# A two-layer decoder trunk on one core: where the forget columns stand in the SyncE queue, and from which count the first three weight loads may start

## What is computed

```python
cond = jax.nn.silu(c)
mod = cond @ w_mod[l] + b_mod[l]                 # (2048) @ (2048, 12288)
sh1, sc1, g1, sh2, sc2, g2 = jnp.split(mod, 6, axis=-1)
h = modulate(rms_norm(x, norm_gain[l, 0]), sh1, sc1)
proj = h @ w_in                                  # w_in: (2048, 3 * 2048 + 8)
q, k, v = proj[..., :3 * D] ...                  # 16 heads of 128
f_logit = proj[..., 3 * D:] + b_forget           # the eight forget columns
```

## Time and profile before

| what | us |
|---|---|
| median of 3 runs | 2072.96 (2072.81 to 2076.98) |
| the profiled execution, whole | 2075.47 |
| its span (first to last instruction) | 2073.9 |
| TensorE busy in it | 2005.1 (97%) |
| VectorE busy | 1655.8 (80%) |
| ScalarE busy | 1054.7 (51%) |
| GpSimd busy | 307.4 (15%) |

### The profile page before, as it was taken

The page is one execution under the profiler, slowest core; times in us unless marked ns, Lnnn a source line. Parts: engine busy times, 40 slices in busy tenths (PEclk is TensorE's granted clock), DMA queues, the critical chain, the costliest instruction groups (busy, mean ns, idle before and its releaser), DMA issues.

```text
span 2073.9 us, 33153 instructions
## 1 busy us (share of the span) xinstructions
PE 2005.1 (97%) x12242; PEld 1792.9 (86%) x12242; DVE 1655.8 (80%) x2321; ACT 1054.7 (51%) x1551; POOL 307.4 (15%) x459
## 2 busy tenths in 40 slices
PE   3999999999999999999999999899999999999998
PEld 2888989888999889999899987688888888888886
DVE  5777899987899998998989986898965666666665
ACT  4323764554555544555445555555543555434553
POOL 3332342220121122111211210011100000000000
PEclk8999999999999999999999999999999999999999
DMA  9999899886789899888998884297765555555552
GB/s 360 355 353 328 305 330 333 298 298 215 257 314 333 319 353 343 321 317 295 353 358 303 313 305 143 88 336 268 262 203 184 194 190 184 199 186 192 194 184 101
DMA packets 235851, 558.39 MB, mean 269 GB/s; under 512 B 14024, under 2 KB 15032, under 8 KB 235192
## 3 DMA queue, kind: packets, MB, share of 16 engines
q1 hardware_dynamic: 180408, 355.03, 49.4%
q0 software_dynamic: 55296, 201.35, 27.3%
HBM read 554.23 MB, written 2.10 MB: 268 GB/s over the span
## 4 chain that ended last, share of the span: by engine, by line
PE 86%; DVE 6%; issue 3%; DMA 3%; ACT 2%; POOL 0%; DVEq 0%; POOLq 0%; ACTq 0%
PE ps L680 15%; PE ps L704 10%; PE ps L706 10%; PE ps L705 10%; PE ps L655 8%; PE ps L657 8%; PE ps L656 8%; PE ps L685 8%; PE ps L724 3%; DVE w_lo L1522 2%; DVE macc L1536 2%; DMA mraw<-in_w_mod 1%; PE ps L721 1%; DMA early<-in_w_mod 1%; ACT work L1108 1%
## 5 line engine op out<-in xcount | busy, mean ns | idle before, releaser
L1108 ACT ACTIVATE w_hi<-raw 128x1024 fp32r<-128x1024 f32 x640 | 668.3, 1057 | 726.6 <-PE ps L706 242.1
L1522 DVE TENSOR_TENSOR w_lo<-raw,w_hi 128x1024 fp32r<-128x1024 f32 x640 | 767.2, 1226 | 296.4 <-ACT w_hi L1108 295.3
L655 PE MATMUL ps<-h_pair,w_hi 128*128 128x256 f32 x1792 | 513.9, 287 | 2.0 <-DVE w_lo L1522 1.6
L656 PE MATMUL ps<-h_pair,w_hi 128*128 128x256 f32 x1792 | 508.5, 284 | 0.0
L657 PE MATMUL ps<-h_pair,w_lo 128*128 128x256 f32 x1792 | 508.4, 284 | 0.0
L1536 DVE SCALAR_TENSOR_TENSOR macc<-mraw,cond,macc 128x512 f32<-128x512 f32 x620 | 427.9, 748 | 47.8 <-DMA mraw<-in_w_mod 39.9
L540 POOL DMA_DIRECT2D mraw<-in_w_mod x358 | 258.8, 723 | 1170.9 <-DVE macc L1536 874.9
L655 PEld LDWEIGHTS ps<-h_pair,w_hi 128*128 128x128 f32 x1792 | 345.1, 193 | 4.8 <-issue 4.7
L656 PEld LDWEIGHTS ps<-h_pair,w_hi 128*128 128x128 f32 x1792 | 345.1, 193 | 1.3 <-issue 1.2
L657 PEld LDWEIGHTS ps<-h_pair,w_lo 128*128 128x128 f32 x1792 | 344.9, 192 | 0.0
L680 PE MATMUL ps<-h_pair,w_hi 128*128 128x512 f32 x1408 | 340.5, 393 | 1.1 <-DVE w_lo L1522 1.0
(11 more groups left out here) (177 smaller groups left out, 1511.5 us busy)
## 6 DMA issues: line engine op xcount, KB each, us to landing
mraw<-in_w_mod POOLq DMA_DIRECT2D x358, 512.0 KB, 6.2
raw<-in_w_up SPq DMA_DIRECT2D x176, 1024.0 KB, 6.1
raw<-in_w_down SPq DMA_DIRECT2D x88, 1024.0 KB, 5.9
raw<-in_w_attn_in SPq DMA_DIRECT2D x48, 1024.0 KB, 8.3
raw<-in_w_attn_out SPq DMA_DIRECT2D x16, 1024.0 KB, 7.2
work<-in_w_mod POOLq DMA_DIRECT2D x12, 512.0 KB, 8.8
early<-in_w_mod POOLq DMA_DIRECT2D x8, 512.0 KB, 12.8
raw<-in_w_pool SPq DMA_DIRECT2D x4, 1024.0 KB, 5.1
```

The costliest lines, as they stand in the source:

```text
L655: mm(o, wh, ah, start=st, stop=False, skip_group_check=True)
L656: mm(o, wh, al, start=False, stop=False, skip_group_check=True)
L1108: return nc.scalar.activation(o, i, f, **kw)
L1522: V.tensor_tensor(w_lo[:, s, :, :], raw[:, j % 4, h * 1024:(h + 1) * 1024].rearrange("p (k n) -> p k n", k=2), w_hi[:, s, :, :].bitcast(F3 ...
```

## The change

The loads of `wf` and `bfb` are taken out of the loop over positions, where they stood ahead of position 4, and put ahead of position 0, directly behind the last parameter load. The loads at positions 0, 1 and 2 wait for `mod_acc` at 16, 20 and 24 in place of 22, 24 and 26: for VectorE to be through with pieces 1, 3 and 5 of chunk 1, where before it had to be through with pieces 4, 5 and 6.

```diff
+            with nc.allow_non_contiguous_dma("the eight forget columns, the bias on every partition"):
+                sp.dma_start(wf[:, :, :], w_attn_in[0, :, 3 * D:3 * D + NF]
+                             .rearrange("(k p) n -> p k n", p=P)).then_inc(s_wf, 16)
+                sp.dma_start(bfb[:, :], b_forget[0:1, :].to_broadcast([P, NF])).then_inc(s_wf, 16)
+
             def load(q, j, src):
 
                 if isinstance(q, int) and q == 0:
-                    sp.wait_ge(mod_acc, (22, 24, 26, 34)[j])
+                    sp.wait_ge(mod_acc, (16, 20, 24, 34)[j])
                     if j >= 2:
                         sp.wait_ge(x_t, 8)
...
             for pos in range(48):
-                if pos == 4:
-                    with nc.allow_non_contiguous_dma("the eight forget columns, the bias on every partition"):
-                        sp.dma_start(wf[:, :, :], w_attn_in[0, :, 3 * D:3 * D + NF]
-                                     .rearrange("(k p) n -> p k n", p=P)).then_inc(s_wf, 16)
-                        sp.dma_start(bfb[:, :], b_forget[0:1, :].to_broadcast([P, NF])).then_inc(s_wf, 16)
```

## The result

The changed kernel takes 2079.18 us (median of 22 runs, 2075.32 to 2084.99), the kernel before, on the same chips, 2074.22 us (median of 22). The ratio is 1.0022, interval 1.0016 to 1.0028: 4.6 us slower, between 3.3 and 5.8. The forecast was 4.6 us slower. One of the 22 runs of the kernel before took 9860.24 us; a median is hardly moved by it. The profiled execution took 2079.26 us against 2075.47, 3.8 us more, with a span of 2077.7 us.

The account below looks back on a forecast made before the run. TensorE, 97% busy, was taken as the bound, its stream starting when the load at position 0 lands. A start at 49.0 in place of 44.39 adds 4.6 us to the median 2072.96: 2077.6 us, 8 in 10 between 2072.9 and 2080.4.

Parts of the forecast that it names:

- Start of the stream: TensorE's first L724, released by the load at position 0: at 49.0 us (47.4 to 50.5), 4.6 us later than 44.39.
- the level engines' 47.4: Landing of the load at position 0 if all engines are level: 44.7 us plus 2.7 us for 1.05 MB, +3.0.
- The lag of 2.0 us: In q0 some engine runs 2.0 us behind, so the load at position 0 lands there at 49.4 us.
- Packets in turn: Engines take one packet from q0 and q1 in turn, whatever its size; 136 small ones each, 0.183 us a turn.
- rival A: Small loads in q1 go in bundles, stream starts 4.1 us earlier, 2068.9 to 2070.9 us; chance 0.12.
- The counts at 0: Earlier wait of the load at position 0: alone at most 4.3 us gained, with the small loads ahead 0.
- The hold of SyncE: Issue of `bfb` holds SyncE's queue from about 11 us to between 33 and 42; cost 0.
- Chunk 2 and the load at position 3: VectorE's wait for piece 4 goes from 3.66 us to about 1; load at position 3 up to 6 us later.
- a cover of 13: Slack before the first product of the load at position 3, behind TensorE's sum at 69.46: 13 us against 6.
- The clock: Low level at TensorE's start rises a like time behind it, so the delay counts full 4.6 us, not half, 2.3.
- Handed on whole: Between 170 and 230 us VectorE follows TensorE, not the transfers, so a later start is passed on in full.
- rival C: The delay is given back through slack or the clock: +1 to +2.5 us, about 2075 us; chance 0.08.

Follow-up runs that it names:

- e3_half: Changed kernel with 8 of 16 rows of `wf` per partition ahead of position 0, the rest and `bfb` ahead of position 4; ratio to kernel before 1.0008.
- e2_move: Changed kernel with the old counts 22, 24, 26, so only `wf` and `bfb` are moved; ratio to the kernel before 1.0021 (1.0013 to 1.0030).
- e1_counts: Kernel before with only the counts changed to 16, 20, 24, `wf` and `bfb` still ahead of position 4; ratio 1.0015 (1.0006 to 1.0023).
- e5_bias_first: Changed kernel with `bfb` issued ahead of `wf` in place of behind it; one run, no ratio, first L724 at 48.94 us.
- e9_pos3_old: Kernel before with `wf` and `bfb` ahead of position 3 in place of 4, counts 22, 24, 26 kept; ratio 1.0010 (1.0001 to 1.0019).
- e6_act: Changed kernel (counts 16, 20, 24) with `wf` on ScalarE's queue at the head of its program, `bfb` ahead of position 0; ratio to kernel before 0.9993.
- e4_quarter: Changed kernel with 4 of 16 rows of `wf` per partition ahead of position 0, the rest and `bfb` ahead of position 4; ratio to kernel before 0.9994.

## Why the prediction was right

*Start of the stream.* Forecast 49.0 (47.4 to 50.5), measured 49.15 in the changed kernel, 49.18 and 48.94 in two others with all packets ahead. The choice of a time near the slowest engine's over the level engines' 47.4 was right, but two terms of the sum were off by about as much in opposite directions, so part of the closeness is luck. For the slow engine the sum has the last run at 46.7 and the load 2.7 us behind it. By the packets of the changed kernel's trace, the last run moves at 45.2, and the load lands 3.9 us behind it. The lag of 2.0 us was read from a landing: in the kernel before q0's last packet moves at 49.2 and lands at 50.0, so 0.8 of the 2.0 is no engine's delay but the way from a last packet to its landing.

*Packets in turn.* Right, and now direct: 905 to 905. The rule of the Trainium skill that was rival A (DMA: Bandwidth & Descriptors, section Queues, rings and completion order: some 9 to 17 descriptors from one ring before switching) doesn't hold for these transfers; by it, as an estimate from the page, 136 small packets would take 8 to 15 turns, at 0.183 us a turn less than 3 us, and `wf` landed at 45.3, 18.9 us behind the parameters' last packet (26.4). The measurement decides. One size was off: I counted a turn as 0.183 us, for q0's packets of 4 KB alone. The rows have 905 turns on 16 engines in 9 us, 0.159 us each, since q0's packets of 4 bytes (104 of the 905) are turns too. There are more turns for as much less time, so the end of q0 doesn't move, but what stands ahead of a load is worked off faster: this is the 1 us by which e3_half was forecast too late (its 64 runs an engine were to end at 38.2 and end at 36.9).

*The counts at 0.* Right in this kernel (e2_move). The value I gave them alone, up to 4.3 us at the start, was right for the start (39.84) and wrong for the end, as e1_counts shows; the prediction didn't rest on it.

*The hold of SyncE.* Forecast to end between 33 and 42 and to cost nothing: it ended at 33.4, and e5_bias_first shows the nothing (48.94 in place of 49.15). That holds for a hold ahead of position 0; in e9_pos3_old, ahead of position 3, one does cost.

*Chunk 2 and the load at position 3.* VectorE's wait for piece 4 was to go from 3.66 to about 1 and went to 0. The load at position 3 was to come up to 6 us later and came 5.9 later, under a cover of 13; no wait of TensorE came of it.

*The clock.* Taken at the full value and not at half: the granted clock rises at 53.7 us, 4.5 us behind the start, and at 49.7 in the kernel before, 5.3 us behind it (the prediction had read 5.7). So of 4.8 us 4.4 are left behind position 1.

*Handed on whole.* Right for a delay: +4.6 in e5_bias_first at every point to 131 us, and +4.4 at 480. The changed kernel's own profile went back to 2.9, because it didn't have the stretch at low clock at 70.6, and to 3.7 later. The range of the timed ratio, 3.3 to 5.8 us, holds the 4.6. This is not rival C: what came back was that stretch at low clock, which isn't in all profiles of either kind, not slack.

The same step would have been wrong for a gain. Of the six profiles (five kernels) whose stream starts at 39.8 to 41.3 only one, e6_act's, kept 3 us, and the second profile of the same kernel kept 0.9. From 60 to 131 us the modulation's chunks and the loads at 3 and 4 follow the transfers, not TensorE, with 13 us or less in hand, and TensorE waits 0.9 to 3.2 us for a chunk in the other five. Where a wait is followed by the low clock, it costs a second time, as the rows at 84 and 120 us show. What sets the other short stretches at low clock (70, 238, 299, 973, 1112 us in some executions) stays open; each is worth some 1.5 us, which is part of what executions of one kernel differ by.

## What to carry to other kernels

A transfer of many short runs is cheap in bytes and costs one turn a run: ahead of a wanted load, on the same queue and beside a full one, count packets per engine, not KB, and price each at the other queue's packet. Leave out those that are gone before the load would move its own first packet, and those that run when the other queue is empty. Put such a transfer where the engines are still empty, on a queue nothing urgent follows on; directly behind the last small loads was the worst of the places tried, since another queue had filled the engines by then. And ask of a gain at the start what else must come earlier for it to last: a delay is handed on by itself, a gain only if every supplier has the slack.

## What I had not expected of the hardware

One us of idle TensorE in the first 130 us can cost twice. In e4_quarter it waits 1.3 us in 116 to 119.2 us, and the next 3.4 us run at a granted clock of 0.57, which costs about as much again. Over all profiles TensorE waits nine times for the sum of chunk 3 or 5. Seven of these waits (1.1 to 3.2 us) have a stretch at the low level beginning 0.6 to 2.2 us behind them; two (0.9 us in e4_quarter, 1.1 us in e9_pos3_old) have none. Between 79 and 131 us no profile has such a stretch without such a wait. No run changed the wait alone, so this is what goes together, not a shown cause.

Not all engines had the same queue ahead. In 10 to 26.5 us q1 moved 1476 packets in the changed kernel and 1122 in the one before: 354 more packets went by while the parameters were still on their way, so some engines were done with the parameters much earlier.

```profile
q0 software_dynamic: 1528, 5.58, 91.8%
q1 hardware_dynamic: 1476, 0.51, 12.7%
```

The Trainium skill (DMA: Bandwidth & Descriptors, section Why a DMA increments its semaphore by 16 and not by 1) says that a DMA is spread over the largest number of engines up to 16 that divides its slowest dimension; for the eight loads of 88 rows that would be 11, with five engines left out. e4_quarter agrees with its numbers. Of its 512 runs ahead of position 0, 32 on each engine, 160 (5 times 32) move between 15.2 and 20.2 us, then none for 6 us, and the other 352 (11 times 32) between 26.2 and 31.7. For the forecast this made no difference, since a landing waits for the engines that come last.
